# Attention probabilities turned by VectorE and 16 SBUF transfers a head, in place of TensorE transposes

## What is computed

```python
logits = jnp.einsum('bqhmd,bkhmd->bhmqk', q_blk, k).astype(f32) * scale + bias[None, :, None]
logits = jnp.where(visible, logits, NEG_INF)        # causal by chunks of 64
p = jax.nn.softmax(logits, axis=-1)
attn = p[:, :, 0] - lam * p[:, :, 1]
return jnp.einsum('bhqk,bkhe->bqhe', attn.astype(v.dtype), v)
```

## Time and profile before

| | |
|---|---|
| Time, median of 3 runs | 1756.7 us (1756.33 to 1756.97) |
| Profiled execution, span from its first to its last instruction | 1754.5 us |
| Median less span | 2.2 us |
| TensorE busy | 1746.8 us |
| VectorE busy | 1269.8 us |
| ScalarE busy | 744.8 us |
| GpSimd busy | 487.5 us |
| Mean granted TensorE clock | 0.999 of full speed |

### The profile page before, as it was taken

The page is one execution under the profiler, slowest core; times in us unless marked ns, Lnnn a source line. Parts: engine busy times, 40 slices in busy tenths (PEclk is TensorE's granted clock), DMA queues, the critical chain, the costliest instruction groups (busy, mean ns, idle before and its releaser), DMA issues.

```text
span 1754.5 us, 21902 instructions
## 1 busy us (share of the span) xinstructions
PE 1746.8 (100%) x8231; PEld 1454.1 (83%) x8231; DVE 1269.8 (72%) x1688; ACT 744.8 (42%) x967; POOL 487.5 (28%) x204
## 2 busy tenths in 40 slices
PE   9999999999999999999999999999999999999998
PEld 7888888888888888888888888888888888888888
DVE  7998767573678777577779787665746797585585
ACT  4234654343564443343432345543445544343343
POOL 4453000103034244444133620010030333444440
PEclk9999999999999999999999999999999999999999
DMA  6532222322322332232231312223222223322321
GB/s 216 192 120 73 103 103 96 127 90 97 119 82 87 122 116 79 98 115 85 107 144 72 145 69 106 103 97 120 97 97 96 97 99 118 121 72 97 120 75 70
DMA packets 30698, 185.97 MB, mean 106 GB/s; under 512 B 3709, under 2 KB 6013, under 8 KB 10241
## 3 DMA queue, kind: packets, MB, share of 16 engines
q1 hardware_dynamic: 28380, 172.71, 27.4%
q0 software_dynamic: 1648, 11.54, 1.7%
q10 hardware_dynamic: 564, 0.33, 0.1%
HBM read 179.25 MB, written 7.68 MB: 107 GB/s over the span
## 4 chain that ended last, share of the span: by engine, by line
PE 96%; DVE 2%; issue 1%; ACT 1%; POOL 0%; DVEq 0%; POOLq 0%; ACTq 0%
PE ps L1640 28%; PE ps L1656 28%; PE ps L1641 28%; PE ps L1582 2%; PE ps L1576 2%; PE ps L1575 2%; PE ps L1739 1%; PE ps L1759 1%; DVE merged L1202 1%; DVE x_tl L985 1%; PE ps L1751 0%; PE ps L1670 0%; PE ps L1891 0%; PE ps L1884 0%; PE ps L1885 0%
## 5 line engine op out<-in xcount | busy, mean ns | idle before, releaser
L1640 PE MATMUL ps<-x_hd,w_hd 128*128 128x512 f32 x1568 | 612.8, 391 | 0.2
L1641 PE MATMUL ps<-x_tl,w_hd 128*128 128x512 f32 x1568 | 610.4, 389 | 0.0
L566 POOL TENSOR_TENSOR w_tl<-raw,w_hd 128x2048 fp32r<-128x2048 f32 x79 | 366.1, 4634 | 534.4 <-ACT w_hd L684 400.7
L684 ACT ACTIVATE w_hd<-raw 128x2048 fp32r<-128x2048 f32 (+2 forms) x159 | 298.2, 1876 | 324.8 <-PE ps L1641 240.3
L1656 PE MATMUL ps<-x_hd,w_tl 128*128 128x512 f32 x1568 | 373.4, 389 | 0.0
L1640 PEld LDWEIGHTS ps<-x_hd,w_hd 128*128 128x128 f32 x1568 | 294.4, 188 | 62.5 <-issue 0.8
L1656 PEld LDWEIGHTS ps<-x_hd,w_tl 128*128 128x128 f32 x1568 | 294.1, 188 | 61.0
L1641 PEld LDWEIGHTS ps<-x_tl,w_hd 128*128 128x128 f32 x1568 | 294.4, 188 | 60.3
L1640 PE MATMUL ps<-ring_hd,w_hd 128*128 128x512 f32 (+1 forms) x640 | 241.1, 381 | 0.0
L1641 PE MATMUL ps<-ring_tl,w_hd 128*128 128x512 f32 (+1 forms) x640 | 239.8, 379 | 0.0
L1347 DVE SCALAR_TENSOR_TENSOR merged<-merged 128x512 f32<-128x512 f32 x44 | 183.3, 4166 | 20.7 <-ACT merged L684 20.3
(11 more groups left out here) (227 smaller groups left out, 1646.1 us busy)
## 6 DMA issues: line engine op xcount, KB each, us to landing
raw<-units SPq DMA_DIRECT2D x154, 1024.0 KB, 4.8
bias_t<-bias_tiles POOLq DMA_DIRECT2D x8, 256.0 KB, 5.5
cg<-mem_t POOLq DMA_DIRECT2D x2, 1024.0 KB, 6.8
resid<-x_t POOLq DMA_DIRECT2D x1, 2048.0 KB, 8.2
resid_dram<-resid POOLq DMA_DIRECT2D x1, 2048.0 KB, 9.1
resid<-resid_dram POOLq DMA_DIRECT2D x1, 2048.0 KB, 8.8
out<-resid SPq DMA_DIRECT2D x7, 256.0 KB, 2.7
resid<-x_t SPq DMA_DIRECT2D x3, 512.0 KB, 9.0
```

Of the source, the lines that this page charges most:

```text
L566: line.done(pool.tensor_tensor(w_tl[:, k % 2, :], raw[:, k % 2, :], w_hd[:, k % 2, :].bitcast(F32), ALU.subtract), of_unit("tail", g))
L684: line.done(act.activation(out, in_, func, **kw), *labels)
L1640: pe.matmul(dst, w_hd[:, slot, w], hd[:, src, :], start=kc == 0, stop=False)
L1641: i = pe.matmul(dst, w_hd[:, slot, w], tl[:, src, :], start=False, stop=False)
```

## The change

TensorE's job C and ACT's copies go. After `combine`, VectorE turns half 0 of `s_sb` into half 1 in one instruction, which transposes every 32 x 32 block in place of the 128 x 128 ones. The output is laid out so that a column's number within its block comes first and the block's number (ten of them) last: element (column q, block t) lies at 10 q + t. Then a full transpose is a swap of groups of 32 partitions with groups of 320 columns. SP does that with 16 transfers of 32 partitions x 320 columns (40 KB each) from half 1 back into half 0, ahead of its load of unit 19 + 3h. Job D waits until all 16 have landed, and reads its stationary blocks from half 0, every tenth column. TensorE's scores of the next head wait for VectorE's reading of the banks (`sc_freeB`) and no longer for ACT's copies.

```diff
-    ATT.setdefault(ATT0 + 3 * _h + 2, []).append(("C", _h))
+TURN_AT = {ATT0 + 3 * _h + 6: _h for _h in range(HEADS)}
-        att_t = s_sb[:, 1, :]
+        att_t = s_sb[:, 0, :].rearrange("p (q t) -> p t q", q=P)
+            def turn(h):
+                sp.wait_ge(vector_done, line.at(f"turned{h}"))
+                for a in range(4):
+                    for b in range(4):
+                        sp.dma_start(s_sb[32 * b:32 * b + 32, 0, 320 * a:320 * a + 320],
+                                     s_sb[32 * a:32 * a + 32, 1, 320 * b:320 * b + 320]).then_inc(att_in, 16)
+
             for g in range(2, TOTAL):
+                line.begin(g // NU)
+                if g % NU in TURN_AT:
+                    turn(TURN_AT[g % NU])
                 sp.wait_ge(gpsimd_done if tail_by_pool(g - 2) else vector_done, line.at(of_unit("tail", g - 2)))
                 sp.dma_start(raw[:, g % 2, :], units[g]).then_inc(weights_in[g % 2], 16)
...
-                        elif job == "C":
-                            for (bank, c0), o, w in (((4, 0), 0, 512), ((5, 0), 512, 384), ((6, 0), 896, 384)):
-                                op(att_t[:, o:o + w], ps[:, bank, c0:c0 + w], labels=(f"att{h}",), needs=(f"C{h}",))
...
-                    free = (f"C{h - 1}", f"D{h - 1}") if h else ()
+                    free = (f"D{h - 1}",) if h else ()
...
+                op(lambda: dve.transpose(s_sb[:, 1, :].rearrange("p (b i t) -> p t b i", b=4, i=32),
+                                         s_sb[:, 0, :].rearrange("p (t b i) -> p t b i", b=4, i=32)), f"turned{h}")
...
-                        pe.wait_ge(scalar_done, line.at(f"att{h - 1}"))
+                        pe.wait_ge(vector_done, line.at(f"sc_freeB_{h - 1}"))
...
-                elif job == "C":
-                    pe.wait_ge(vector_done, line.at(f"probs{h}"))
-                    for kb in range(TB):
-                        bank, c0 = AT_AT[kb]
-                        for qb in range(kb, TB):
-                            c = c0 + P * (qb - kb)
-                            s0 = SO[qb] + P * kb
-                            i = pe.transpose(ps[:, bank, c:c + P], s_sb[:, 0, s0:s0 + P], ident[:])
-                    line.done(i, f"C{h}")
                 elif job == "D":
-                    pe.wait_ge(scalar_done, line.at(f"att{h}"))
+                    pe.wait_ge(att_in, 256 * (l * HEADS + h + 1))
...
-                            c = AO[kb] + P * (qb - kb)
-                            i = pe.matmul(misc[:, P * qb:P * qb + P], att_t[:, c:c + P], v_sb[:, kb, P * h:P * h + P],
+                            i = pe.matmul(misc[:, P * qb:P * qb + P], att_t[:, SO[qb] // P + kb], v_sb[:, kb, P * h:P * h + P],
...
-                        pe.wait_ge(scalar_done, line.at("att3"))
+                        pe.wait_ge(vector_done, line.at("sc_freeB_3"))
```

More of the change, by code:

```diff
@@ L254 @@
 YA_ROUNDED = CLN + 5
-AO = [0, 512, 896, 1152]
-AT_AT = [(4, 0), (5, 0), (6, 0), (6, 256)]
+TURN_AT = {ATT0 + 3 * _h + 6: _h for _h in range(HEADS)}
 C_IN, C_OUT = (0, 1, 4, 5), (2, 3, 0, 6)
@@ L449, in build @@
             sem("wsbs_in"), sem("resid_out"), sem("resid_in"), sem("mem_in"))
+        att_in = sem("att_in")
         bias_in = [sem("bias_in0"), sem("bias_in1")]
@@ L1119, in combine @@
                     op(lambda: dve.scalar_tensor_tensor(s0, s1, rc[:, 4 + qb:5 + qb], s0, ALU.mult, ALU.add),
-                       f"probs{h}", independent=min(qb, 1))
+                       independent=min(qb, 1))
+                op(lambda: dve.transpose(s_sb[:, 1, :].rearrange("p (b i t) -> p t b i", b=4, i=32),
+                                         s_sb[:, 0, :].rearrange("p (t b i) -> p t b i", b=4, i=32)), f"turned{h}")
             def conv_taps(taps):
```

## The result

| | before | after |
|---|---|---|
| Time, median of 4 runs | 1756.72 us (1756.33 to 1756.97) | 1775.27 us (1774.89 to 1775.96) |
| Span of the profiled execution | 1754.5 us | 1773.5 us |
| Mean granted TensorE clock | 0.999 | 0.997 |
| TensorE busy | 1746.8 us | 1758.1 us |

The change costs 18.6 us: ratio 1.0108, 95% interval 1.0094 to 1.0121. The prediction was 9.9 us slower, 1747.5 to 1785.5.

What follows compares the result with a forecast made beforehand. TensorE, busy 1746.8 of 1754.5 us, was taken as the bound. 1756.7 - 8.7 (transposes) + 0 (VectorE) + 0.8 (transfers) + 17.8 (loads) = 1766.6 us, range 1747.5 to 1785.5.

Steps and rivals of the forecast that it cites:

- The transposes, -8.7 us: TensorE's ten transposes a head, 1.09 us in each of eight places, leave its path: 8.7 us less.
- VectorE's turning, 2.5 us, covered: One VectorE instruction over 1280 columns a head, between combine and evacuation, taken at 2.5 us; idle gaps hide it, 0 us.
- The stationary operand, +17.8 us: The 160 loads for products with the values read columns 40 bytes apart; pair time doubles, 160 x 0.1115 us.
- the doubling: Spread stationary loads rule and take twice a pair's time, anything from half to one and a half times 17.8 us; chance 0.36.
- the argument from the middle of the range: Stationary loads cost between 0 and 30.7 us; the middle is 15.4, and twice a pair's time, 17.8 us, is next to it.
- The transfers, +0.8 us: Sixteen SP transfers a head make TensorE wait 0.4 us before head 0's products in each layer; other heads covered.
- combine's end + turning + issues + landing: When the last block lands: combine's end + 2.5 + 0.1 + 15 x 0.46 + 2.2 = +11.7 us, set against TensorE's arrival.
- The weight load behind the transfers: Head 0's next weight load on SP's queue is issued at about 200.9, lands by 206; ACT takes it at 214.40, covered.
- Free stride: Rival: the load of a spread operand still fits beside the product, so no stride cost; 1748.8 us, chance 0.34.
- The transfers as the new path: Rival: slower issue and landing make TensorE wait in all heads, 25 us in all; 1773 us with no stride cost, chance 0.12.
- four cases: Chances: loads doubled or so 0.36, stride free 0.34, three times the pitch 0.18, transfers as the path 0.12.
- What would show it: Expected signs: twenty products at 2.23, 4.5 or 6.7 us a head, load record above 0.192, TensorE idle in head 0 only.

Runs made afterwards that it cites:

- half the transfers: Kernel after the change with only 8 of its 16 transfers a head, the other blocks left unmoved, stationary step of ten kept: 1765.4 us, ratio 1.0051.
- two queues: Kernel after, with blocks interleaved in pairs (stationary step 2) and GpSimd issuing six of head 0's sixteen transfers, SP ten: 1748.5 us, ratio 0.9956 to before.
- head 0 on TensorE: Kernel after with blocks interleaved in pairs for heads 1 to 3, head 0 keeping TensorE's transposes and ACT's copies: 1751.7 us, ratio 0.9974 to before.
- contiguous blocks: Kernel after, but its products with the values read stationary blocks from 128 adjacent columns (wrong elements), turning and 16 transfers kept: 1760.3 us, ratio 1.0021 to before.
- the version with VectorE alone: Kernel after without transfers: VectorE does sixteen 32 x 320 transposes a head straight into place, stationary blocks contiguous: 1776.1 us, ratio 1.0112 to before.
- the measured steps: Kernel before, its products with the values reading stationary blocks every second, third, fourth or tenth column: 1757.1, 1765.6, 1774.8 and 1773.9 us.
- layout of pairs: Kernel after with the ten blocks interleaved in pairs, so stationary step 2; VectorE turns in two instructions: 1756.3 us, ratio 0.9997 to before.

## Why the prediction was right, and where it was not

It was right in sign and in the mechanism of its largest term, and gave about half of the size: +9.9 us forecast, +18.6 measured. By its own steps:

- *The transposes, -8.7 us.* Right. Nothing waited behind them: with that figure the sums above close within 0.1 us (half the transfers, two queues), 0.7 us (head 0 on TensorE) and about 2 us (contiguous blocks).
- *VectorE's turning, 2.5 us, covered.* 2.58 us, and no wait of TensorE names VectorE in the attention. That the cover ends was shown by the version with VectorE alone. The turning takes 2.58 us / 1280 = 2.0 ns a column at a step of ten elements, and 1.65 / 1280 = 1.3 ns at a step of two. The Trainium skill, page "Vector Engine (DVE) Microarchitecture Reference", section 5.2, has 2.50 ns a column for an output that steps 24 words; the prediction's estimate from it, 3.2 us, is too high for this instruction.
- *The stationary operand, +17.8 us.* Right in size as well as mechanism: 17.7 us measured alone. That it came out within 0.1 us is luck: the doubling was picked between bounds far apart, and the argument from the middle of the range carries no weight of its own; the rows of before held nothing that could tell 9 from 18 or from 30. What the measured steps add is where the slack ends: a load that touches 64 lines still all but hides beside its product.
- *The transfers, +0.8 us.* This is the mis-sized term: 9.9 us measured, by taking half of them away. Of the formula "combine's end + turning + issues + landing" the structure held, one entry didn't. The issue was taken at 0.46 us from four issues at the start of the kernel; sixteen in a row take 10.08 us, 0.63 each. Landing was 1.9 us for 2.2. With these, 2.6 + 15 x 0.63 + 1.9 + 0.1 = 14.1 us for 11.7, and the prediction's own arrival times give 190.87 + 14.1 - 202.2 = 2.8 us in head 0 (measured 2.79) and 306.45 + 14.1 - 320.0 = 0.6 in head 3 (0.51). The range of 0.33 to 0.75 us had held the value; 0.17 us too little, fifteen times, less what landing gave back, made 2.4 us at each head 0, and uncovered head 3 in both layers. A nearer row lay in the trace of before: the four small transfers that the earlier trace rows give as 0.75 us each are three of 0.60 and one of 1.06.

```profile
L526 SPq DMA_DIRECT2D bias_tiles<-neg_tile x4: 596/598/1060, 63.3 to 65.7; - x4
```

  The two waits that are left, 0.25 us in head 1 of layer 0 and 0.56 in head 2 of layer 1, come with single long issues. In the first the sixteen take 10.68 us where head 2's take 10.02; in the second one issue takes 1.84 us (SP in order of time, then the chain):

```profile
234.15 10.68 SPq L531 DMA_DIRECT2D s_sb<-s_sb  x16
275.14 10.02 SPq L531 DMA_DIRECT2D s_sb<-s_sb  x16
...
1155.72 1.84 SPq L531
```

  With 10.02 us neither wait would be there. Why one issue is long at times stays open.
- *Around the waits.* Left out altogether: each wait costs about 0.4 us more than its idle time, 2.5 us in six. And the clock, of which the prediction said that a pause of a microsecond or two gave it no reason to expect otherwise, fell after one of 2.8 us. With strided loads that hardly shows (0.1 us); with contiguous ones it is 1.7 us a time.
- *The weight load behind the transfers.* Right: it is issued at 203.95 in place of 194.75 and ScalarE doesn't wait for it.

The account of the kernel after is then -8.7 + 17.7 + 7.4 + 2.5 = +18.9 us, against 18.6 measured. Its last two terms together are the 9.9 us measured with half the transfers; how they divide is read from the trace.

The rivals. "Free stride" with 1748.8 us was wrong twice: the stride isn't free, and the kernel after with contiguous blocks measures 1760.3. "The transfers as the new path" came with its deciding point of 0.65 us an issue, and the runs show 0.63: with contiguous blocks they do eat the gain and a little more. So two of the four cases held at once, which the sum over separate cases could not give. What would show it was mostly there: blocks of 4.5 us, records over 0.192, a transpose between the bounds; idle time "under 1 us, head 0 only" was not, and the text had said what that would mean.

## What to carry to other kernels

Price a stationary operand by the 16-byte lines that its columns touch: here two fp32 elements a line hid beside the product and one a line doubled its time, which a layout of pairs avoids for 0.1 us a head. A row of small transfers on one queue is a serial stretch, here of about 0.63 us each plus a landing, so set its whole length against the reader's arrival and, where it is too long, split it over a second queue. And a stall of TensorE costs more than its idle time: here 0.3 to 0.4 us for starting anew, and up to 1.7 more where the clock falls.

## What the hardware did that I had not expected

The granted clock fell to its lower level after waits of 2.3 to 3.3 us in head 0, and gave 1.7 us away in a block of 2.4; but not after one of 3.08 us in layer 1 of the layout of pairs. In the version with VectorE alone it fell around the four waits of 2.42 to 4.20 us and stayed at the upper level after those of 1.01 and 1.89. A block ruled by strided loads took nearly the same time at either level (4.84 and 4.91 us at a mean granted clock of 0.64 and 0.69, 4.81 at full). The issue of a transfer took 0.59 us in both shapes of 40 KB, against 0.33 for the lone load of the earlier trace rows, and 0.58 for the load right behind the sixteen. VectorE's transpose of 32 partitions and 320 columns took 0.50 us, 1.6 ns a column, where all 128 partitions together took 1.3 to 2.0.
